# Two weight sums of a Strassen step added by DMA transfers of GpSimd's queue, and the reopened product moved from sixth to third

## The chip, the cores and the metric

One core of one Trainium2 chip runs the whole kernel. The metric is the time of one execution on the device in microseconds; the kernel before has a median of 2315.39 us over 3 runs (2314.23 to 2316.02).

## What is computed

One layer of a hybrid encoder: a modulated RMS norm, two kinds of attention, an output projection, then a second norm and a SwiGLU feed-forward part, all in float32. The change touches the feed-forward part alone:

```python
h2 = rms_norm(x, norm2_g[layer]) * (1 + sc2[:, None]) + sh2[:, None]
ff = (jax.nn.silu(h2 @ w_gate[layer]) * (h2 @ w_up[layer])) @ w_down[layer]
x = x + g2[:, None] * ff
```

Here h2 is 512 x 2048, w_gate and w_up are 2048 x 5632, and w_down is 5632 x 2048.

## The kernel before, in words

Each float32 operand is held as two float32r parts, "hi" and "lo" (lo = full - hi), and each product is three matmuls: hi by hi, hi by lo, lo by hi. ScalarE (ACT) makes the hi part of a weight tile with a Copy, and VectorE (DVE) makes the lo part with a subtraction.

The 5632 columns of w_gate and w_up are done in 44 tiles of 128 (f = 0 to 43). The first 4 (NPL) are done plainly. The other 40 are done by a Strassen-Winograd step that turns eight half products into seven. In the program a tile f >= 4 is a **set** (`product_set` on each engine), and one of its seven products is a **form**, numbered i = 0 to 6 by its place in the set. A form is 8 k-tiles x 3 matmuls = 24 matmuls of 256 columns. Six of the seven activation-side operands are ready-made (H, or the combinations T1 to T4, made once); the weight-side operands are four pieces of 128 x 1024 float32 (512 KB) that SyncE (SP) loads into `raw` slots 0 to 3, and four sums of them.

In a set of the kernel before, DVE makes the four sums in place (`add_raw`, L1783): raw0 += raw2, raw2 += raw3, raw3 += raw0, raw1 += raw3, where each name means the slot's content at that moment. `FORM_RAW` says which raw slot a form is split from, and `FORM_SLOT` where its hi and lo parts go (slots 0 and 1 in W, 3 and 4 in the free half columns of H). Counting semaphores carry the order: `hi_done` and `lo_done` count the halves of the split, `used` counts forms that TensorE (PE) has finished, `summed` counts sums, `raw_in[slot]` landings.

PE takes the forms in the order of the banks P0, P1, S0, S1, T0, P0 again (opened again and added to: the product B21), T1. The combination afterwards is the **u chain** of DVE (L1834 to L1841, five subtractions and additions of 128 x 256): it needs bank T0, and is released by `used` when the T0 form is done. It frees P1 and S1 and leaves the up half and one quarter of the gate to be finished: `c_12` (L1806, needs T1), `silu_11` (ACT L1197, needs the reopened P0), `silu_12` (ACT L1201), and `f_product` (L1811), whose 256 KB result `ftile` GpSimd (POOL) stores to DRAM (`store_f`, L2040). The queue of each engine is written out by hand, so an instruction that waits holds all behind it. In DVE's queue the first split of the next set (`split_form(f, 0)`) stands behind the u chain of the set before.

After the last set the down projection starts (`down_pair`), with the stored f tiles loaded back by POOL (`load_f`, L2049) into the T tiles and H as the last forms free them, and split again (`f_high` on ACT, `f_low` on DVE, L1851).

Of the kernel before, what the change touches and what calls it, by code (L numbers as in the profile page):

```python
# [36 lines left out]
FT = FF // P  # L37
# [6 lines left out]
NPL = 4  # L44
# [37 lines left out]
def layer(nc, x, c, w_ada, b_ada, norm1_g, w_first, w_in, rpb, na_g, lam_p, sub_g, t5, w_out, norm2_g, w_gu, w_down,  # L82
          final_g, out):
    ctx = ExitStack()
    with ctx:
# [3 lines left out]
        def sem(name):  # L89
            return ctx.enter_context(nc.semaphore(name))  # L90
# [138 lines left out]
        gated, f_made, f_hi = sem("gated"), sem("f_made"), sem("f_hi")  # L229
        t_step, t_hi, t_lo = sem("t_step"), sem("t_hi"), sem("t_lo")  # L230
        summed, p1_kept, u_made = sem("summed"), sem("p1_kept"), sem("u_made")
        c12_made, gate_a, gate_b = sem("c12_made"), sem("gate_a"), sem("gate_b")
        f_stored, f_ready = sem("f_stored"), sem("f_ready")
        f_in = [sem(f"f_in{i}") for i in range(7)]
# [24 lines left out]
            return raw_part(slot).rearrange("p (k c) -> p k c", c=HS)  # L259

        FORM_SLOT = (0, 1, 3, 4, 0, 1, 3)
        FORM_RAW = (0, 3, 0, 2, 3, 1, 1)

        def form_no(f, i):
            return NF * f + (STR0 - NF * NPL + i)
# [36 lines left out]
        def landings(slot, group):  # L302

            return 16 * group + 16 * (3, 3, 4, 4, 1 - NK, 1 - NK)[slot]
# [50 lines left out]
        def _(sp):  # L355
# [144 lines left out]
                sp.wait_ge(lo_done, STR0 - 4 + j + 1)  # L500
                load_form(NPL, slot)
            with sp.Fori(NPL + 1, FT) as f:
                sp.wait_ge(summed, 4 * f + (3 - 4 * (NPL + 1)))
                load_form(f, 0)
                sp.wait_ge(lo_done, form_no(f, 4 - NF))
                load_form(f, 2)
                sp.wait_ge(summed, 4 * f + (4 - 4 * (NPL + 1)))
                load_form(f, 3)
                sp.wait_ge(lo_done, form_no(f, 0))
                load_form(f, 1)  # L510
# [5 lines left out]
                cols = down_cols(q, by_row)  # L516
                load(q % 4, w_down[bass.ds(row, 1)].rearrange("a p n -> (a p) n")[:, k0:k0 + cols], cols)

            sp.wait_ge(summed, 4 * FS - 1)
            load_down(0, 0, 0)  # L520
            sp.wait_ge(lo_done, DOWN0)
            load_down(0, 0, 1)
            load_down(0, 0, 2)
            sp.wait_ge(summed, 4 * FS)
            load_down(0, 0, 3)
            for q in range(4, 8):
                sp.wait_ge(lo_done, down_no(0, 0, q - 3))
# [19 lines left out]
        def _(pe):  # L547
# [249 lines left out]
            def form(f, i, bank, rhs, start=True, reopen=False):  # L797

                pe.wait_ge(lo_done, form_no(f, i + 1))
                wh, wl = form_parts(FORM_SLOT[i])  # L800
                out = bank[:, 0:HS]
                for j in range(HALF):
                    hi, lo = [w[:, j // 2, (j % 2) * P:(j % 2) * P + P] for w in (wh, wl)]
                    xh, xl = rhs[j]
                    pe.matmul(out, hi, xh, start=start and j == 0, stop=False, skip_group_check=reopen)  # L805
                    pe.matmul(out, hi, xl, start=False, stop=False, skip_group_check=reopen)  # L806
                    mm = pe.matmul(out, lo, xh, start=False, stop=j == HALF - 1, skip_group_check=reopen)  # L807
                mm.then_inc(used, 1)

            def product_set(f, first=False):  # L810
                pe.wait_ge(gated, NPL) if first else pe.wait_ge(gate_a, f - NPL)
                form(f, 0, Pb[0], B11, reopen=True)
                if first:
                    pe.wait_ge(f_made, NPL)
                    pe.wait_ge(t_lo, 4 * HALF)
                else:
                    pe.wait_ge(u_made, 5 * f - 5 * NPL)
                form(f, 1, Pb[1], T4c)
                form(f, 2, Sb[0], T3c)
                form(f, 3, Sb[1], T1c)  # L820
                form(f, 4, Tb[0], T2c)
                pe.wait_ge(p1_kept, f - (NPL - 1))
                form(f, 5, Pb[0], B21, start=False, reopen=True)
                if not first:
                    pe.wait_ge(c12_made, f - NPL)
                form(f, 6, Tb[1], B22)
# [46 lines left out]
        def _(act):  # L873
# [318 lines left out]
                    split_loaded(NPL, 0, STR0 - 1)  # L1192

            def silu_11(f):
                act.wait_ge(used, form_no(f, 6))
                act.wait_ge(f_made, f)
                act.activation(gate[:, 0:HS], Pb[0][:, 0:HS], ACT.Silu).then_inc(gate_a, 1)  # L1197

# [4 lines left out]
            def product_set(f, first=False):  # L1203
                if not first:
                    split_loaded(f, 0, form_no(f, -2))
                    silu_11(f - 1)
                split_loaded(f, 1, form_no(f, 0 if first else -1))
                split_form(f, 2, summed, 4 * f + (1 - 4 * NPL), form_no(f, 0))
                if not first:
                    silu_12(f - 1)  # L1210
                split_form(f, 3, summed, 4 * f + (2 - 4 * NPL), form_no(f, 0))
                act.wait_ge(used, form_no(f, 1))
                if not first:
                    act.wait_ge(u_made, 5 * f - (5 * NPL + 4))
                act.activation(p1s, Pb[0][:, 0:HS], ACT.Copy).then_inc(p1_kept, 1)
                split_form(f, 4, summed, 4 * f + (3 - 4 * NPL), form_no(f, 1))
                split_loaded(f, 5, form_no(f, 2))
                split_form(f, 6, summed, 4 * f + (4 - 4 * NPL), form_no(f, 3))

            product_set(NPL, True)  # L1220
            with act.Fori(NPL + 1, FT) as f:
# [13 lines left out]
                      down_cols(q, by_row), slot_free)  # L1235

            split_down(0, 0, 0, slot_free=3)
            silu_11(FT - 1)
            f_high(0, 1, 2, 3)
            split_down(0, 0, 1, slot_free=3)  # L1240
            f_high(4, 5)
# [29 lines left out]
        def _(dve):  # L1271
# [541 lines left out]
            def product_set(f, first=False):  # L1813
                g5 = 5 * f - 5 * NPL
                if not first:
                    split_form(f, 0)
                dve.wait_ge(raw_in[2], landings(2, f + GRP0))
                add_raw(0, 0, 2)
                split_form(f, 1)
                if not first:  # L1820
                    c_12(f - 1)
                add_raw(2, 2, 3)
                if not first:
                    f_product(f - 1)
                split_form(f, 2)
                add_raw(3, 3, 0)
                split_form(f, 3)
                split_form(f, 4)
                split_form(f, 5)
                add_raw(1, 1, 3)  # L1830
                split_form(f, 6)
                dve.wait_ge(used, form_no(f, 5))
                dve.wait_ge(p1_kept, f - (NPL - 1))
                dve.tensor_tensor(u2, Tb[0][:, 0:HS], p1s, ALU.subtract).then_inc(u_made, 1)  # L1834
                dve.wait_ge(u_made, g5 + 1)
                dve.tensor_tensor(u3, u2, Sb[0][:, 0:HS], ALU.subtract).then_inc(u_made, 1)
                dve.tensor_tensor(u4, u2, Sb[1][:, 0:HS], ALU.add).then_inc(u_made, 1)
                dve.wait_ge(u_made, g5 + 2)
                dve.wait_ge(f_stored, 16 * f)
                dve.tensor_tensor(ftile[:, 0:HS], u3, Pb[1][:, 0:HS], ALU.add).then_inc(u_made, 1)  # L1840
                dve.tensor_tensor(ftile[:, HS:S], u3, Sb[1][:, 0:HS], ALU.add).then_inc(u_made, 1)  # L1841
# [74 lines left out]
        def _(pool):  # L1916
# [131 lines left out]
                land = triple[2][:, k * S:(k + t1 - t0) * S].rearrange("p (t n) -> p t n", n=S)  # L2048
                pool.dma_start(land, f_d.ap()[t0:t1].rearrange("t p n -> p t n")).then_inc(f_in[r % 7], 16)  # L2049

            with pool.Fori(0, FT - 1) as f:
                store_f(f)
            for r, n in enumerate((DOWN0 - 4, DOWN0 - 3, DOWN0 - 3, DOWN0 - 2, DOWN0, DOWN0, DOWN0)):
                load_f(r, n)
            store_f(FT - 1)
            pool.wait_ge(x_new, KT + 1)
# [54 lines left out]
```

## Time and profile before

| | |
|---|---|
| median of 3 runs | 2315.39 us (2314.23 to 2316.02) |
| the profiled execution | 2317.39 us, its span 2315.5 us |
| PE busy | 2256.2 us (97%) |
| DVE busy | 1578.2 us (68%) |
| ACT busy | 850.6 us (37%) |
| POOL busy | 264.1 us (11%) |
| moved by DMA | 357.02 MB |

"Busy" adds up the instructions of an engine in the profiled execution; the span runs from its first instruction to its last. The matmuls overlap, so PE's share says only that it nearly always had one in hand; how fast it goes is read from the distance between their starts. The stage with the 40 sets runs from about 1009 to 1816 us of the span.

### The profile page before, as it was taken

What the parts mean: (1) busy time and instruction counts of PE and PEld (TensorE: products, weight loads), DVE (VectorE), ACT (ScalarE), POOL (GpSimd) and SP (SyncE); (2) the same over time, 40 slices, a digit from 0 to 9 for tenths busy, and PEclk for the clock granted to TensorE, in tenths of its full rate; (3) what the DMA queues carried; (4) which work ended last, traced back from release to release, by engine and by line L of the source; (5) the groups of instructions that cost most, each with busy time, mean ns of one, the idle gap of its engine ahead of it and who ended that gap; (6) DMA issues with size and microseconds to landing.
All of it is one profiled execution on the core that took longest, in us unless ns stands there. A gap on an engine that the chain in (4) does not pass through costs nothing.

```text
span 2315.5 us, 36235 instructions
## 1 busy us (share of the span) xinstructions
PE 2256.2 (97%) x13160; PEld 1968.7 (85%) x13160; DVE 1578.2 (68%) x2158; ACT 850.6 (37%) x1210; POOL 264.1 (11%) x268
## 2 busy tenths in 40 slices
PE   7989999999999998999999999999999999999997
PEld 5878788777777887799999999999999888888885
DVE  6886777766776898777777777877777632243334
ACT  4224433344445213434444444444434422232221
POOL 4012332200003332000000000000000100001111
PEclk9999999999999998999999999999999999999998
DMA  9896666533442984233333333333333633353333
GB/s 337 285 349 173 199 194 189 188 125 120 163 143 92 353 288 165 91 112 114 110 114 122 122 122 117 113 116 109 117 122 122 225 96 97 94 171 95 99 94 109
DMA packets 126615, 357.02 MB, mean 154 GB/s; under 512 B 12809, under 2 KB 37529, under 8 KB 126049
## 3 DMA queue, kind: packets, MB, share of 16 engines
q1 hardware_dynamic: 115282, 318.03, 41.1%
q0 software_dynamic: 10272, 38.08, 5.5%
q8 instruction: 32, 0.52, 0.1%
q10 hardware_dynamic: 1008, 0.21, 0.1%
q14 instruction: 21, 0.17, 0.0%
HBM read 337.09 MB, written 19.18 MB: 154 GB/s over the span
## 4 chain that ended last, share of the span: by engine, by line
PE 91%; DVE 4%; DMA 2%; ACT 1%; POOL 1%; issue 1%; DVEq 0%; SPq 0%; ACTq 0%; POOLq 0%
PE P L552 7%; PE P L554 7%; PE P L553 7%; PE P L805 5%; PE P L806 5%; PE P L807 5%; PE S L849 3%; PE T L849 3%; PE T L848 3%; PE S L850 3%; PE S L848 3%; PE T L850 3%; PE T L807 3%; PE T L806 3%; PE T L805 3%; PE S L807 3%
## 5 line engine op out<-in xcount | busy, mean ns | idle before, releaser
L1276 DVE TENSOR_TENSOR W_lo<-raw,W_hi 128x1024 fp32r<-128x1024 f32 (+2 forms) x256 | 283.5, 1107 | 331.7 <-ACT W_hi L879 330.9
L879 ACT ACTIVATE W_hi<-raw 128x1024 fp32r<-128x1024 f32 (+2 forms) x256 | 236.8, 925 | 569.9 <-PE T L850 179.5
L552 PE MATMUL P<-H_hi,W_hi 128*128 128x512 f32 x832 | 341.5, 410 | 20.9 <-POOL ident L1948 9.2
L554 PE MATMUL P<-H_hi,W_lo 128*128 128x512 f32 x832 | 326.9, 393 | 0.0
L553 PE MATMUL P<-H_lo,W_hi 128*128 128x512 f32 x832 | 326.4, 392 | 0.0
L1172 ACT ACTIVATE W_hi<-raw 128x1024 fp32r<-128x1024 f32 x160 | 169.2, 1058 | 217.2 <-PE T L807 155.3
L552 PEld LDWEIGHTS P<-H_hi,W_hi 128*128 128x128 f32 x832 | 157.4, 189 | 68.6 <-issue 21.1
L1780 DVE TENSOR_TENSOR W_lo<-raw,W_hi 128x1024 fp32r<-128x1024 f32 x160 | 194.4, 1224 | 3.3 <-ACT W_hi L1172 2.9
L1783 DVE TENSOR_TENSOR raw<-raw 128x1024 f32<-128x1024 f32 x160 | 195.0, 1219 | 0.0
L1172 ACT ACTIVATE H_hi<-raw 128x1024 fp32r<-128x1024 f32 x120 | 127.2, 1060 | 175.5 <-DVE raw L1783 115.2
L554 PEld LDWEIGHTS P<-H_hi,W_lo 128*128 128x128 f32 x832 | 157.1, 189 | 34.3
L553 PEld LDWEIGHTS P<-H_lo,W_hi 128*128 128x128 f32 x832 | 157.7, 190 | 30.7 <-issue 1.9
L805 PE MATMUL S<-T_hi,H_hi 128*128 128x256 f32 x640 | 181.1, 283 | 0.0
L806 PE MATMUL S<-T_lo,H_hi 128*128 128x256 f32 x640 | 181.1, 283 | 0.0
L807 PE MATMUL S<-T_hi,H_lo 128*128 128x256 f32 x640 | 181.1, 283 | 0.0
L806 PE MATMUL P<-H_lo,W_hi 128*128 128x256 f32 x640 | 181.1, 283 | 0.0
L807 PE MATMUL P<-H_hi,W_lo 128*128 128x256 f32 x640 | 181.1, 283 | 0.0
L805 PE MATMUL P<-H_hi,W_hi 128*128 128x256 f32 x640 | 181.1, 283 | 0.0
L1780 DVE TENSOR_TENSOR H_lo<-raw,H_hi 128x1024 fp32r<-128x1024 f32 x120 | 146.6, 1222 | 48.1 <-ACT H_hi L1172 48.1
L2040 POOL DMA_DIRECT2D f_d<-gf x44 | 23.9, 544 | 880.3 <-DVE gf L1811 770.8
L806 PEld LDWEIGHTS P<-H_lo,W_hi 128*128 128x128 f32 x640 | 122.9, 192 | 0.0
L805 PEld LDWEIGHTS P<-H_hi,W_hi 128*128 128x128 f32 x640 | 122.9, 192 | 0.0
(245 smaller groups left out, 5448.0 us busy)
## 6 DMA issues: line engine op xcount, KB each, us to landing
raw<-in_w_gu SPq DMA_DIRECT2D x176, 512.0 KB, 3.3
raw<-in_w_in SPq DMA_DIRECT2D x72, 512.0 KB, 4.3
adar<-in_w_ada SPq DMA_DIRECT2D x72, 512.0 KB, 4.4
att<-in_w_ada SPq DMA_DIRECT2D x32, 1024.0 KB, 10.9
att<-in_w_ada SPq DMA_DIRECT2D x56, 512.0 KB, 4.8
raw<-in_w_down SPq DMA_DIRECT2D x64, 384.0 KB, 3.1
raw<-in_w_down SPq DMA_DIRECT2D x64, 320.0 KB, 2.9
raw<-in_w_out SPq DMA_DIRECT2D x32, 512.0 KB, 4.9
```

The source lines that it names most:

```text
L552: pe.matmul(bank[:, :], wh, xh, start=start, stop=False)
L553: pe.matmul(bank[:, :], wh, xl, start=False, stop=False)
L554: return pe.matmul(bank[:, :], wl, xh, start=False, stop=stop)
L805: pe.matmul(out, hi, xh, start=start and j == 0, stop=False, skip_group_check=reopen)
L806: pe.matmul(out, hi, xl, start=False, stop=False, skip_group_check=reopen)
L807: mm = pe.matmul(out, lo, xh, start=False, stop=j == HALF - 1, skip_group_check=reopen)
L848: pe.matmul(banks[b][:, :], hi, xh, start=(p == 0 and j == 0), stop=False)
L879: act.activation(w_parts(slot)[0][:, 0:cols], raw[:, raw_slot * PW:raw_slot * PW + cols], ACT.Copy).then_inc(hi_done, 1)
L1172: act.activation(form_parts(FORM_SLOT[i])[0], raw_form(FORM_RAW[i]), ACT.Copy).then_inc(hi_done, 1)
L1276: dve.tensor_tensor(lo[:, 0:cols], raw[:, raw_slot * PW:raw_slot * PW + cols], hi[:, 0:cols].bitcast(F32), ALU.subtract).then_inc(lo_done, 1)
L1780: dve.tensor_tensor(lo, raw_form(FORM_RAW[i]), hi.bitcast(F32), ALU.subtract).then_inc(lo_done, 1)
L1783: dve.tensor_tensor(raw_part(dst), raw_part(a), raw_part(b), ALU.add).then_inc(summed, 1)
```

## The change

On POOL, each set now begins with two transfers that add a weight piece from DRAM onto the piece in a raw slot (`accum_op=ALU.add`): raw2 += piece 3 once raw2 has landed, counted by `s1_in`, and raw0 += piece 2 once form 0 of the same set has been split, counted by `s3_in`. The store of the tile before stands behind both. DVE loses two of its four `add_raw`. The reopened product (B21, from raw1) becomes form 2, and the forms of S0, S1 and T0 become 3, 4 and 5; `silu_11` moves into its own set, and the reloads at the end wait for the new form numbers.

```diff
-        FORM_RAW = (0, 3, 0, 2, 3, 1, 1)
+        FORM_RAW = (0, 3, 1, 0, 2, 3, 1)
...
             with sp.Fori(NPL + 1, FT) as f:
-                sp.wait_ge(summed, 4 * f + (3 - 4 * (NPL + 1)))
+                sp.wait_ge(summed, 2 * f + (1 - 2 * (NPL + 1)))
                 load_form(f, 0)
-                sp.wait_ge(lo_done, form_no(f, 4 - NF))
+                sp.wait_ge(lo_done, form_no(f, 5 - NF))
                 load_form(f, 2)
-                sp.wait_ge(summed, 4 * f + (4 - 4 * (NPL + 1)))
+                sp.wait_ge(summed, 2 * f + (2 - 2 * (NPL + 1)))
                 load_form(f, 3)
...
                 form(f, 1, Pb[1], T4c)
-                form(f, 2, Sb[0], T3c)
-                form(f, 3, Sb[1], T1c)
-                form(f, 4, Tb[0], T2c)
                 pe.wait_ge(p1_kept, f - (NPL - 1))
-                form(f, 5, Pb[0], B21, start=False, reopen=True)
+                form(f, 2, Pb[0], B21, start=False, reopen=True)
+                form(f, 3, Sb[0], T3c)
+                form(f, 4, Sb[1], T1c)
+                form(f, 5, Tb[0], T2c)
...
             def silu_11(f):
-                act.wait_ge(used, form_no(f, 6))
+                act.wait_ge(used, form_no(f, 3))
...
                     split_loaded(f, 0, form_no(f, -2))
-                    silu_11(f - 1)
                 split_loaded(f, 1, form_no(f, 0 if first else -1))
-                split_form(f, 2, summed, 4 * f + (1 - 4 * NPL), form_no(f, 0))
+                split_loaded(f, 2, form_no(f, 0))
                 if not first:
                     silu_12(f - 1)
-                split_form(f, 3, summed, 4 * f + (2 - 4 * NPL), form_no(f, 0))
...
-                split_form(f, 4, summed, 4 * f + (3 - 4 * NPL), form_no(f, 1))
-                split_loaded(f, 5, form_no(f, 2))
-                split_form(f, 6, summed, 4 * f + (4 - 4 * NPL), form_no(f, 3))
+                split_form(f, 3, s3_in, 16 * f + (16 - 16 * NPL), form_no(f, 0))
+                split_form(f, 4, s1_in, 16 * f + (16 - 16 * NPL), form_no(f, 1))
+                split_form(f, 5, summed, 2 * f + (1 - 2 * NPL), form_no(f, 2))
+                silu_11(f)
+                split_form(f, 6, summed, 2 * f + (2 - 2 * NPL), form_no(f, 3))
...
                     split_form(f, 0)
-                dve.wait_ge(raw_in[2], landings(2, f + GRP0))
-                add_raw(0, 0, 2)
                 split_form(f, 1)
                 if not first:
                     c_12(f - 1)
-                add_raw(2, 2, 3)
+                split_form(f, 2)
                 if not first:
                     f_product(f - 1)
-                split_form(f, 2)
+                split_form(f, 3)
                 add_raw(3, 3, 0)
-                split_form(f, 3)
                 split_form(f, 4)
                 split_form(f, 5)
                 add_raw(1, 1, 3)
                 split_form(f, 6)
-                dve.wait_ge(used, form_no(f, 5))
+                dve.wait_ge(used, form_no(f, 6))
...
-            with pool.Fori(0, FT - 1) as f:
+            def add_weights(f):
+
+
+                def add(slot, other, landed):
+                    pool.dma_start(raw_part(slot), w_gu[bass.ds(4 * f + other, 1)].rearrange("a p n -> (a p) n"),
+                                   accum_op=ALU.add).then_inc(landed, 16)
+
+                pool.wait_ge(raw_in[2], landings(2, f + GRP0))
+                add(2, 3, s1_in)
+                pool.wait_ge(lo_done, form_no(f, 1))
+                add(0, 2, s3_in)
+
+            with pool.Fori(0, NPL - 1) as f:
                 store_f(f)
-            for r, n in enumerate((DOWN0 - 4, DOWN0 - 3, DOWN0 - 3, DOWN0 - 2, DOWN0, DOWN0, DOWN0)):
+            with pool.Fori(NPL, FT) as f:
+                add_weights(f)
+                store_f(f - 1)
+            for r, n in enumerate((DOWN0 - 3, DOWN0 - 2, DOWN0 - 3, DOWN0 - 1, DOWN0, DOWN0, DOWN0)):
                 load_f(r, n)
```

`form_no(f, n)` as a value of `used` or `lo_done` means that forms 0 to n-1 of set f are through.

On PE, in the loop over the sets, the last part of a set: the T0 form (operand T, weights in W), then the reopened P form, then the T1 form (T<-H_hi: weights and operand both in H). Before:

```order
L805 MATMUL T<-T_hi,W_hi 128x256 [waits lo_done]
...
L799 REGISTER_ALU [waits p1_kept]
L805 MATMUL P<-H_hi,W_hi 128x256 [waits lo_done]
...
L799 REGISTER_ALU [waits c12_made]
L805 MATMUL T<-H_hi 128x256 [waits lo_done]
```

Now, from the reopened P form on:

```order
L800 REGISTER_ALU [waits p1_kept]
L806 MATMUL P<-H_hi 128x256 [waits lo_done]
...
L806 MATMUL S<-T_hi,H_hi 128x256 [waits lo_done]
...
L806 MATMUL S<-T_hi,W_hi 128x256 [waits lo_done]
...
L806 MATMUL T<-T_hi,W_hi 128x256 [waits lo_done]
...
L800 REGISTER_ALU [waits c12_made]
L806 MATMUL T<-H_hi 128x256 [waits lo_done]
```

Two forms stood between the end of T0's form and the first form of the next set; now there is one.

On DVE, the end of the loop body (the u chain, after which the body begins anew with the first split and what follows it). Before, the end:

```order
L1833 REGISTER_ALU [waits used]
L1834 TENSOR_TENSOR tail<-T,tail 128x256 [waits p1_kept]
L1835 ISA
L1836 TENSOR_TENSOR tail<-tail,S 128x256 [waits u_made]
L1837 TENSOR_TENSOR tail<-tail,S 128x256
L1838 REGISTER_ALU
L1839 REGISTER_ALU [waits u_made]
L1840 TENSOR_TENSOR gf<-tail,P 128x256 [waits f_stored]
L1841 TENSOR_TENSOR gf<-tail,S 128x256
```

and the beginning of the body, before:

```order
L1780 TENSOR_TENSOR W_lo<-raw,W_hi 128x1024 [waits hi_done]
L1817 ISA
L1783 TENSOR_TENSOR raw<-raw 128x1024 [waits raw_in2]
L1778 REGISTER_ALU
L1780 TENSOR_TENSOR W_lo<-raw,W_hi 128x1024 [waits hi_done]
```

and now:

```order
L1780 TENSOR_TENSOR W_lo<-raw,W_hi 128x1024 [waits hi_done]
L1778 REGISTER_ALU
L1780 TENSOR_TENSOR W_lo<-raw,W_hi 128x1024 [waits hi_done]
L1804 ISA
L1805 ISA [waits used]
L1806 TENSOR_TENSOR tail<-T,tail 128x256 [waits u_made]
```

The end of the body is the same five operations in the same place of DVE's queue; only the form that its wait names has moved. From the beginning, the first sum is gone.

On POOL, the loop over the sets, now (before, it held the last three rows and the loop's own):

```order
L2052 ISA [waits raw_in2]
L2052 DMA raw<-in_w_gu 128x1024
L2057 ISA
L2052 ISA [waits lo_done]
L2052 DMA raw<-in_w_gu 128x1024
L2037 ISA [waits f_made]
L2037 DMA f_d<-gf 128x512
L2062 REGISTER_ALU
```

Two waits and two transfers now stand ahead of the store.

## Rows read from the trace of the kernel before

**Rows 1.** Busy time by stretch: us; busy us of PE, PEld, DVE, ACT, POOL; clock, DMA share, GB/s

```profile
1014.00:1100.00 86.00, 86.00 (x719) 86.00 (x718) 69.34 (x78) 36.69 (x44) 2.17 (x4) 1.00 0.36 122
1100.00:1780.00 680.00, 680.00 (x5670) 680.00 (x5668) 527.53 (x609) 283.06 (x338) 18.43 (x34) 1.00 0.35 116
1830.00:1900.00 70.00, 70.00 (x310) 57.98 (x309) 27.36 (x37) 21.08 (x32) 0.53 (x1) 1.00 0.38 119
```

**Rows 2.** PE's waits from 1009 to 1830 us: waited for, us in total, times, longest

```profile
PE P L805 <- DVE W_lo L1780: 0.3, 1, 0.3
```

**Rows 3.** Groups of instructions by form, 1100 to 1780 us (33.7 sets)

```profile
L1783 DVE TENSOR_TENSOR raw<-raw 128x1024 f32<-128x1024 f32 x136 | 165.7, 1219 | 0.0
```

**Rows 4.** PE's timeline in one set: last T0 matmul, first reopened P, first T1

```profile
1306.48 0.28 PE L807 MATMUL T<-T_hi,W_lo 128*128 128x256 f32 x1
1306.60 0.28 PE L805 MATMUL P<-H_hi,W_hi 128*128 128x256 f32 x1
...
1309.48 0.28 PE L805 MATMUL T<-H_hi 128*128 128x256 f32 x1
```

**Rows 5.** DVE's timeline in the same set: u chain, first split of the next set

```profile
1306.89 0.43 DVE L1834 TENSOR_TENSOR tail<-T,tail 128x256 f32<-128x256 f32 x1 [2.84 <-PE T L807]
1307.35 0.42 DVE L1836 TENSOR_TENSOR tail<-tail,S 128x256 f32<-128x256 f32 x1
...
1308.35 0.41 DVE L1841 TENSOR_TENSOR gf<-tail,S 128x256 f32<-128x256 f32 x1
1308.68 1.22 DVE L1780 TENSOR_TENSOR W_lo<-raw,W_hi 128x1024 fp32r<-128x1024 f32 x1
```

**Rows 6.** DVE's timeline where the first set begins

```profile
1010.27 1.22 DVE L1783 TENSOR_TENSOR raw<-raw 128x1024 f32<-128x1024 f32 x1
1011.41 1.22 DVE L1780 TENSOR_TENSOR W_lo<-raw,W_hi 128x1024 fp32r<-128x1024 f32 x1
```

**Rows 7.** PE's timeline at the same place

```profile
1012.16 0.28 PE L807 MATMUL P<-H_hi,W_lo 128*128 128x256 f32 x1
1012.77 0.35 PE L805 MATMUL P<-T_hi,W_hi 128*128 128x256 f32 x1 [0.33 <-DVE W_lo L1780]
1012.97 0.28 PE L806 MATMUL P<-T_lo,W_hi 128*128 128x256 f32 x1
```

**Rows 8.** ACT's and DVE's timelines: a sum, the hi half of its split, the lo half

```profile
1300.39 1.22 DVE L1783 TENSOR_TENSOR raw<-raw 128x1024 f32<-128x1024 f32 x1
1301.72 1.06 ACT L1172 ACTIVATE H_hi<-raw 128x1024 fp32r<-128x1024 f32 x1 [2.50 <-DVE raw L1783]
1302.82 1.23 DVE L1780 TENSOR_TENSOR H_lo<-raw,H_hi 128x1024 fp32r<-128x1024 f32 x1 [1.21 <-ACT H_hi L1172]
```

**Rows 9.** DVE's and POOL's timelines: the product of a tile and its store

```profile
1314.13 0.69 DVE L1811 TENSOR_TENSOR gf<-gf 128x512 f32<-128x512 f32 x1
1315.46 0.54 POOL L2040 DMA_DIRECT2D f_d<-gf  x1 [19.61 <-DVE gf L1811]
```

**Rows 10.** DMA issues over the whole span: KB each, median us from issue to landing

```profile
raw<-in_w_gu SPq DMA_DIRECT2D x176, 512.0 KB, 3.3
f_d<-gf POOLq DMA_DIRECT2D x44, 256.0 KB, 2.3
T_f<-f_d POOLq DMA_DIRECT2D x5, 1024.0 KB, 8.0
X<-in_x POOLq DMA_DIRECT2D x4, 1024.0 KB, 6.0
att<-t_d POOLq DMA_DIRECT2D x8, 448.0 KB, 3.8
```

**Rows 11.** DVE's and POOL's timelines where the last set ends and down begins

```profile
1812.68 0.95 DVE L1276 TENSOR_TENSOR W_lo<-raw,W_hi 128x768 fp32r<-128x768 f32 x1
1814.61 2.50 DVE L1851 TENSOR_TENSOR T_lo<-T_f,T_hi 128x512 fp32r<-128x512 f32 x4 [0.98 <-ACT T_hi L1228]
...
1805.30 0.78 POOL L2049 DMA_DIRECT2D T_f<-f_d  x1 [5.45 <-PE S L807]
```

**Rows 12.** PE's timeline there: first matmuls of down

```profile
1816.36 0.40 PE L848 MATMUL S<-T_hi,W_hi 128*128 128x512 f32 x1
1816.59 0.40 PE L849 MATMUL S<-T_lo,W_hi 128*128 128x512 f32 x1
```

**Rows 13.** How long POOL is busy with an issue: duration ns min/median/max

```profile
L2040 POOL DMA_DIRECT2D f_d<-gf x44: 539/542/604, 946.1 to 1822.7; - x44
```

More of the change, by code:

```diff
@@ L231, in layer @@
         summed, p1_kept, u_made = sem("summed"), sem("p1_kept"), sem("u_made")
+        s3_in, s1_in = sem("s3_in"), sem("s1_in")
         c12_made, gate_a, gate_b = sem("c12_made"), sem("gate_a"), sem("gate_b")
@@ L517, in load_down @@
                 load(q % 4, w_down[bass.ds(row, 1)].rearrange("a p n -> (a p) n")[:, k0:k0 + cols], cols)
-            sp.wait_ge(summed, 4 * FS - 1)
+            sp.wait_ge(summed, 2 * FS - 1)
             load_down(0, 0, 0)
@@ L523, in _ @@
             load_down(0, 0, 2)
-            sp.wait_ge(summed, 4 * FS)
+            sp.wait_ge(summed, 2 * FS)
             load_down(0, 0, 3)
@@ L1237, in _ @@
             split_down(0, 0, 0, slot_free=3)
-            silu_11(FT - 1)
             f_high(0, 1, 2, 3)
```

## The prediction

> **What bounds the kernel now.** I read the busy time by stretch first. Through the stage of the 40 sets PE is busy all of the time at a granted clock of 1.00, which is the 2.4 GHz level, while DVE has 78% and the DMA engines 35% [rows 1]. PE starts 5670 matmuls in 680 us, one every 0.120 us [rows 1], so a form of 24 takes 2.88 us (the timeline agrees: 1309.48 - 1306.60 [rows 4]) and a set of 168 takes 20.16 us. Next PE's waits: from 1009 to 1830 us it waited once, 0.3 us [rows 2]. So PE's queue alone sets the time here, and nothing that unburdens DVE can shorten a set. The change leaves PE's 168 matmuls as they are; it can only leave the stage alone or put waits into it. The question is how near each supplier now comes to PE.
>
> **Sums taken off DVE.** Two `add_raw` a set at 1.22 us [rows 3] are 2.4 us less for DVE, in every one of 40 sets. They lie beside PE's work, so I cost them at nothing. One of them counts once: where the first set begins, the sum and the split behind it run from 1010.27 to 1012.63 [rows 6], and PE starts its next form at 1012.77 where its rhythm of 0.12 behind 1012.16 would have had 1012.28, and the matmul after it at 1012.97 instead of 1012.40 [rows 7]. Without the sum that is gone: **-0.6 us**.
>
> These rows also give the price of a late split. It ended 0.35 us after PE wanted to start (1012.63 against 1012.28), and PE lost 0.57. So lost time = lateness + 0.22 us.
>
> **The u chain, moved nearer to the next set.** This is the term that decides. The chain waits for T0's form. Before, that form was the fifth of seven, with two forms (5.76 us) ahead of the next set; now it is the sixth, with one (2.88 us). DVE's queue is in order, and behind the chain stands the lo half of the next set's first split, for which PE's next form waits. What that takes, counted from the start of the form behind T0's: the chain starts 0.29 us later (1306.89 - 1306.60 [rows 4, 5]), its five operations take 1.79 (1308.68 - 1306.89), and the split 1.22 [rows 5]: 0.29 + 1.79 + 1.22 = 3.30 us. Before, 5.76 were there, a margin of 2.46. Now there are 2.88, so the split is 0.42 us late and PE loses 0.42 + 0.22 = **0.64 us at each border between sets, 39 times: +25.0 us**. The hi half on ACT is no help and no harm: its slot is free after the fifth form, as before, and it is done before DVE comes to it. Bounds: if only the lateness counted, 39 x 0.42 = 16 us; if the chain met another 0.25 us of waiting, 39 x 0.89 = 35 us.
>
> **The sum in raw0, added by POOL.** It can be issued only when form 0 has been split, and form 3 is made from it. I count from the end of form 0's split, which now also starts PE's set, 0.22 us later in effect. PE wants form 3 at 0.22 + 8.64 = 8.86. Back from there: 0.14 from a split's end to PE (1012.77 - 1012.63), 1.22 for the lo half, 0.04 between, 1.06 for the hi half, 0.11 from a result to ACT [rows 6, 7, 8]. It must have landed by 6.3. POOL starts an issue 0.64 us after what it waited for (1315.46 - 1314.82 [rows 9]). That leaves **5.6 us from issue to landing**. No row shows an adding transfer. Below stands the plain 512 KB load from the same tensor, 3.3 us; above, a POOL transfer of 1024 KB, 6.0 us, and one of 8.0 where the DMA engines were crowded [rows 10], since an addition has to read the 512 KB in SBUF as well as those in DRAM. POOL's 448 KB took 3.8 [rows 10]. The rate of this queue between 448 and 1024 KB, (6.0 - 3.8) / 576 KB, makes 512 KB 4.0 us. Reading twice as much would bring it to 6.0; with half of the second reading hidden beside the first it is 5.0. I take 5.0, nearer to the 448 KB row because these transfers fall where SP's queue rests, and so cost the wait nothing; the ends are 3.3 and 8.0, which is +0 and 39 x 2.4 = +94 us.
>
> The Trainium skill (DMA: Bandwidth & Descriptors, Anatomy of one DMA) puts a transfer of this queue at 2.0 us and bytes over 436 GB/s: 3.2 us for 512 KB and 4.4 for twice as much; the trace has 6.0 where it gives 4.4 for 1024 KB, so it runs low here. By it the sum of terms would be the same, with 1.2 us to spare.
>
> **The sum in raw2.** Issued when piece 2 of the next set has landed. That load now waits for form 4's split, some 9 to 10 us into a set, so it lands near 13, and even at 8.0 us the sum is there by 22, while form 4 is wanted at 11.5 + 20.8 = 32. Nothing.
>
> **Other moves.** POOL's store stands behind two more issues of about 0.54 us [rows 13]; both are out before `f_product`, and the u chain asks for the store 17 us later. Nothing. The kept copy of P0 must be ready for form 2 at 5.76: form 0 ends at 2.88 and ACT has only `silu_12` before it. Nothing, with over 2 us of cover. `silu_11` leaves the set border, where nobody waited for it. SP's four loads come between 8.5 and 14.5 us into a set and land 3.3 later; the last, raw1, near 18, is wanted after the next border. Nothing. The traffic rises by 1 MB a set, from 35% to some 50 to 60% of the DMA engines.
>
> **The end of the stage.** Behind the last u chain come the first down split (0.95 us for 768 columns) and f tiles at 0.6 each (four in 2.50) [rows 11]. Down's first tile is ready 0.29 + 1.79 + 0.95 + 0.62 = 3.65 us after the last form starts, against 2.88: lost 0.77 + 0.22 = 1.0. Tiles 4 and 5 stand behind one more split and cost about 0.5. The reload of the first four tiles goes out one form (2.88 us) later than at 1805.30; with 8.0 us it lands about 0.2 us before down begins, and may cost another 0.5. Together **+2.0** (0.4 to 5).
>
> **Sum.** 25.0 + 2.0 - 0.6 = +26.4 us. Against the profiled execution, 2317.39, that is 2343.8; the median of the runs lies 2.0 lower, so **2341.8 us**. Its own range is 2332 to 2352.
>
> **Rivals.**
> *The sum in raw0 comes late.* A second wait then joins the first in every set, at form 3. For: the addition's own rate is unknown, and only 0.6 us lie between my 5.0 and the 5.6. At twice the plain load, 6.6 us, PE loses 1.0 more a set: +39, 2381 us. At 8.0 it is 2436.
> *The chain hides after all.* If the chain and the split together took under 2.7 us, for instance because one of the five operations' own waits (0.46 us from the first to the second against 0.33 for the others) is shorter now, the border would cost nothing: 2316 to 2320. Against it: the rows before show the same five operations with the same inputs.
> *Faster.* PE's matmuls of 256 columns start every 0.120 us, while those of 512 columns in down start every 0.226 (70 / 310 [rows 1]; 0.23 [rows 12]), half of which is 0.113. If the difference came from DVE's sums reading and writing SBUF beside PE, taking away half of them could give back up to 168 x 0.007 = 1.2 us a set, 47 us in all, and with the u chain's price 2294. It decides where the distance is shorter while DVE rests. But from 1304.05 to 1306.89 DVE rested [rows 5, 8], and the starts at 1306.48 and 1306.60 in that rest are 0.12 apart all the same [rows 4]. The Trainium skill (TensorE: Matmul & The Clock Gate, Back-to-back issue gap) has columns over 2.4 GHz plus 2.5 ns, 0.109 us for 256; the trace has 0.120.
> That the change doesn't do what it says is out: DVE's order has two sums a set fewer and POOL's two transfers more.
>
> **Chances.** Forecast 0.55; late sum 0.30; hidden chain 0.10; faster 0.05. A difference under 0.2% (4.6 us) can't be told from none. The first two are slower: 0.85. The range runs from 2327, below the forecast's own low end by some of a partly hidden chain, to 2390, which takes in the late sum up to 6.8 us.
>
> **What the profile will show.** Right: in PE's waits a row for the lo split of W with 39 entries of about 0.4 us; sets 20.8 us apart; DVE idle before the u chain for longer than the 2.84 us of before [rows 5]; the adding transfers at about 5 us. Wrong: PE waiting for H's lo half (form 3), which is the late sum; or sets at 20.16; or a distance of matmuls under 0.12.

## The result, and the profile after

| | before | after |
|---|---|---|
| median of 4 runs | 2315.11 us (2314.23 to 2316.02) | 2368.38 us (2358.28 to 2374.32) |
| the profiled execution | 2317.39 us, span 2315.5 | 2366.78 us, span 2365.2 |

The ratio is 1.0226 (95% interval 1.0189 to 1.0262): the changed kernel is 53 us slower. Its runs also spread over 16 us, where those of before lie within 2. The prediction was 2341.8 us, its range 2327 to 2390.

The table of busy time by stretch for the changed kernel, in the same 680 us as in [rows 1] (us; busy us of PE, PEld, DVE, ACT, POOL; clock, DMA share, GB/s):

```profile
1100.00:1780.00 680.00, 653.38 (x5333) 642.60 (x5333) 425.54 (x510) 260.66 (x317) 73.43 (x95) 1.00 0.66 159
```

PE started 5333 matmuls in the stretch instead of 5670: it got through 6% less work, at the same granted clock of 1.00. DVE fell from 528 to 426 us, and the DMA engines' share rose from 0.35 to 0.66. Where PE's time went is in its waits from 1009 to 1880 us (waited for, us in total, times, longest), which were one of 0.3 us before [rows 2]:

```profile
PE S L806 <- DVE H_lo L1780: 20.2, 21, 1.5
PE P L806 <- DVE W_lo L1780: 12.3, 39, 0.3
PE S L849 <- DVE T_lo L1848: 0.9, 2, 0.7
PE P L806 <- DVE H_lo L1780: 0.9, 3, 0.5
```

The second row is the forecast wait, at the border between sets, 39 times. The first is a wait of another kind: the S bank with its weights split into H is form 3, the one made from the raw0 that GpSimd's queue adds to. It came 21 times, up to 1.5 us each. The last row, 3 times and 0.9 us in all, is form 2 (the P bank with its weights in H), which is split from the raw1 that SP loads.

PE's timeline at a border and, further on in the same set, at form 3:

```profile
1328.63 0.28 PE L808 MATMUL T<-H_hi,H_lo 128*128 128x256 f32 x1
1329.22 0.39 PE L806 MATMUL P<-H_hi,W_hi 128*128 128x256 f32 x1 [0.32 <-DVE W_lo L1780]
1329.44 0.28 PE L807 MATMUL P<-H_lo,W_hi 128*128 128x256 f32 x1
...
1339.25 0.39 PE L806 MATMUL S<-T_hi,H_hi 128*128 128x256 f32 x1 [1.13 <-DVE H_lo L1780]
```

In its rhythm of 0.12 PE would have started at 1328.75 and 1328.87; it started at 1329.22 and 1329.44, so the border took 0.57 us. The wait recorded in brackets, 0.32, is shorter: it counts from the recorded end of the matmul before (1328.63 + 0.28 = 1328.91) and not from when the next should have started, and the second matmul starts 0.22 behind the first instead of 0.12.

The starts of the u chain show how this adds up. DVE's timeline (three sets):

```profile
1284.70 0.43 DVE L1831 TENSOR_TENSOR tail<-T,tail 128x256 f32<-128x256 f32 x1 [2.36 <-PE T L808]
...
1305.42 0.43 DVE L1831 TENSOR_TENSOR tail<-T,tail 128x256 f32<-128x256 f32 x1 [2.30 <-PE T L808]
...
1326.16 0.43 DVE L1831 TENSOR_TENSOR tail<-T,tail 128x256 f32<-128x256 f32 x1 [2.29 <-PE T L808]
...
1348.27 0.43 DVE L1831 TENSOR_TENSOR tail<-T,tail 128x256 f32<-128x256 f32 x1 [2.02 <-PE T L808]
```

The first two distances are 20.72 and 20.74 us: a set of before (20.16) and a border (0.57). The third is 22.11: 1.4 us more, the late form 3. (The first matmul of a set starts 3.1 us behind the start of the chain before it, here at 1329.22, and in the set before at 1308.49.) From 1024.51, the first chain, to 1838.96, the 39th, are 814.45 us. At 20.16 a set 38 sets are 766.1; borders take 38 x 0.57 = 21.7, which leaves **26.7 us for late sums** (with the three waits at form 2 among them). In 16 of the 38 distances there is none (20.72 to 20.84 us), in the others 0.4 to 1.8 us.

What the sum in raw0 waited for is in the timelines of POOL and ACT around that late set. POOL's:

```profile
1324.32 0.87 POOL L2052 DMA_DIRECT2D raw<-in_w_gu  x1 [11.40 <-DMA raw<-in_w_gu]
1329.80 0.87 POOL L2052 DMA_DIRECT2D raw<-in_w_gu  x1 [4.61 <-DVE W_lo L1780]
```

ACT's:

```profile
1332.22 1.06 ACT L1173 ACTIVATE H_hi<-raw 128x1024 fp32r<-128x1024 f32 x1 [4.94 <-DMA raw<-in_w_gu]
...
1336.88 1.06 ACT L1173 ACTIVATE H_hi<-raw 128x1024 fp32r<-128x1024 f32 x1 [3.02 <-DMA raw<-in_w_gu]
```

The addition into raw2 went out at 1324.32, the one into raw0 at 1329.80, and its hi split started at 1336.88, when it had landed: about 7.1 us after its issue. The split at 1332.22 is form 2's, which waited for SP's load of raw1. All three transfers were under way together. From issue to landing these two additions took (the smaller is raw0's, the larger raw2's):

```profile
DMA to landing us min/median/max: 7.1/7.5/8.0
```

So raw2's was still in flight for 2.5 us when raw0's went out. The rows of DMA issues, over the whole span (KB each, median us from issue to landing), against 3.3 for SP's before [rows 10]:

```profile
raw<-in_w_gu SPq DMA_DIRECT2D x176, 512.0 KB, 4.3
raw<-in_w_gu POOLq DMA_DIRECT2D x80, 512.0 KB, 7.4
```

The 7.4 is the median over both places. Taken apart in the trace, by the order of issue, the additions into raw2 took 5.4/7.9/8.9 us (min/median/max) and those into raw0, for which form 3 waits, 5.2/6.2/7.5, where I had taken 5.0 and had found room for 5.6. Over the 40 of them, what goes beyond 5.6 us adds up to 29 us, close to the 26.7 lost. When raw0's addition went out, raw2's had 2.4 us still to go at the median.

### The profile page after: what moved, and what is told of

Read it like the earlier page. It is cut to its first block, busy times and chain, and to the rows that moved or that the text cites. A ratio compares the mean times of both kernels' runs of the same rounds, so it can differ in the third digit from the quotient of the medians.

```text
span 2365.2 us, 36358 instructions
## 1 busy us (share of the span) xinstructions
PE 2272.3 (96%) x13160; PEld 1971.7 (83%) x13160; DVE 1483.3 (63%) x2078; ACT 843.2 (36%) x1210; POOL 334.1 (14%) x348
## 4 chain that ended last, share of the span: by engine, by line
PE 75%; DMA 9%; DVE 8%; issue 4%; ACT 2%; POOL 2%; DVEq 0%; POOLq 0%; ACTq 0%; SPq 0%
PE P L553 7%; DMA raw<-in_w_gu 7%; PE P L555 7%; PE P L554 7%; PE S L806 3%; PE T L850 3%; PE T L851 3%; PE T L849 3%; PE S L849 3%; PE S L850 3%; PE S L851 3%; PE S L808 3%; PE S L807 3%; PE P L806 2%; PE T L553 2%
## 5 line engine op out<-in xcount | busy, mean ns | idle before, releaser
L553 PEld LDWEIGHTS P<-H_hi,W_hi 128*128 128x128 f32 x832 | 157.4, 189 | 68.5 <-issue 20.7
L554 PEld LDWEIGHTS P<-H_lo,W_hi 128*128 128x128 f32 x832 | 157.7, 190 | 30.5 <-issue 1.9
L2052 POOL DMA_DIRECT2D raw<-in_w_gu x80 | 69.6, 869 | 590.0 <-DMA raw<-in_w_gu 390.9
L1285 DVE CUSTOM_DVE_ANT_0 adar<-adar,csb 128x1024 f32<-128x1024 f32 x72 | 95.8, 1345 | 35.1 <-DMA adar<-in_w_ada 35.0
L806 PE MATMUL S<-T_hi,H_hi 128*128 128x256 f32 x320 | 92.9, 290 | 20.3 <-DVE H_lo L1780 20.2
L806 PE MATMUL P<-H_hi,W_hi 128*128 128x256 f32 x320 | 94.5, 295 | 12.3 <-DVE W_lo L1780 12.3
L553 PE MATMUL T<-H_hi,W_hi 128*128 128x512 f32 x256 | 99.9, 390 | 1.5 <-DVE W_lo L1276 1.2
L555 PE MATMUL T<-H_hi,W_lo 128*128 128x512 f32 x256 | 99.6, 389 | 0.0
L554 PE MATMUL T<-H_lo,W_hi 128*128 128x512 f32 x256 | 99.6, 389 | 0.0
L1783 DVE TENSOR_TENSOR raw<-raw 128x1024 f32<-128x1024 f32 x80 | 97.5, 1218 | 0.0
```

The source lines that it names most:

```text
L553: pe.matmul(bank[:, :], wh, xh, start=start, stop=False)
L554: pe.matmul(bank[:, :], wh, xl, start=False, stop=False)
L555: return pe.matmul(bank[:, :], wl, xh, start=False, stop=stop)
L1783: dve.tensor_tensor(raw_part(dst), raw_part(a), raw_part(b), ALU.add).then_inc(summed, 1)
```

## The experiments

Each kernel ran beside the kernel before on the same chip. Times are medians; the interval is that of the ratio to the kernel before.

### e1: the new order alone

Edit: the forms in the changed order, all four sums on DVE, no transfer from GpSimd's queue but the store. (Here and below the waits of SP and ACT that count sums change to match; those lines are not shown.)

```diff
                 if not first:
                     split_form(f, 0)
+                dve.wait_ge(raw_in[2], landings(2, f + GRP0))
+                add_raw(0, 0, 2)
                 split_form(f, 1)
                 if not first:
                     c_12(f - 1)
+                add_raw(2, 2, 3)
                 split_form(f, 2)
...
-                pool.wait_ge(raw_in[2], landings(2, f + GRP0))
-                add(2, 3, s1_in)
-                pool.wait_ge(lo_done, form_no(f, 1))
-                add(0, 2, s3_in)
+                pass
```

> The new order of the forms alone: the reopened product third, T0's form sixth, all four sums on DVE and no adding transfer. Theory (the u chain stands too near to the next set): 39 borders lose the 0.57 us that the changed kernel shows where nothing else is late (sets 20.73 us apart instead of 20.16), so about +22 us, 2337 us, and no wait at the S forms. Rival (all of the loss comes from the adding transfers): within 3 us of the kernel before, 2315.

Measured: 2339.30 us, ratio 1.0101 (1.0084 to 1.0118), 24.0 us over the kernel before. PE's waits:

```profile
PE P L806 <- DVE W_lo L1780: 12.5, 40, 0.3
PE S L849 <- DVE T_lo L1851: 1.2, 2, 0.7
```

No wait at an S form is left. 40 waits for W's lo half are the 39 borders and the one where the first set begins, which was there before. So the border is a cost of the order of the forms, with nothing of the transfers in it: 39 x 0.57 = 22.2 of the 24.0 us; the rest is at the end of the stage.

### e2, e3, e7, e8: which transfer, and what of it

e2: both transfers as plain copies (neither sum is computed).

```diff
-                    pool.dma_start(raw_part(slot), w_gu[bass.ds(4 * f + other, 1)].rearrange("a p n -> (a p) n"),
-                                   accum_op=ALU.add).then_inc(landed, 16)
+                    pool.dma_start(raw_part(slot), w_gu[bass.ds(4 * f + other, 1)].rearrange("a p n -> (a p) n")).then_inc(landed, 16)
```

> The changed kernel with the two transfers of GpSimd's queue as plain copies of the same pieces to the same places (the sums raw0 + piece 2 and raw2 + piece 3 are not computed). Theory A (the addition in the transfer is what makes it slow): issue to landing falls from 7.4 to about 4.0 us, no wait at form 3, the u chain's 22 us stay: 2337 us. Theory B (the second queue's traffic alone is enough): landing stays over 6 us and the time near 2368.

e3: only the sum in raw0 on GpSimd's queue.

```diff
                     c_12(f - 1)
+                dve.wait_ge(raw_in[2], landings(2, f + GRP0))
+                add_raw(2, 2, 3)
                 split_form(f, 2)
...
-                pool.wait_ge(raw_in[2], landings(2, f + GRP0))
-                add(2, 3, s1_in)
                 pool.wait_ge(lo_done, form_no(f, 1))
                 add(0, 2, s3_in)
```

> The changed kernel with only the sum in raw0 added by GpSimd's queue; DVE adds the one in raw2. Theory (the two adding transfers get in each other's way and in that of the raw1 load): the remaining one takes about 5.2 us as in the best sets of the changed kernel, no wait at form 3, 2337 us. Rival (one adding transfer is slow by itself): it takes 7 us, PE waits about 1.5 us at form 3 in every set, over 2380 us.

e7 and e8: both transfers, one of them a plain copy (`ALU.bypass`): in e7 the one into raw0, in e8 the one into raw2 (the sum of the plain one is not computed).

> The changed kernel with the transfer into raw0 a plain copy (that sum is not computed) and the one into raw2 adding. Theory (an addition takes 5.3 us alone and only an adding neighbour or the raw1 load stretches it): the adding one 6 us or more beside SP's loads, the plain one about 4.5, no wait at form 3: 2339 us. Rival (the slow part is whatever comes second in the queue, adding or not): form 3 waits as in the changed kernel, near 2360 us.

> The changed kernel with the transfer into raw2 a plain copy (that sum is not computed) and the one into raw0 adding. Theory (it takes an adding neighbour to make the sum in raw0 late): as e3_s3_only, about 5.3 us from issue to landing in the sets, PE waits at form 3 in few sets if any, 2340 us. Rival (the second transfer's traffic does it): form 3 waits in half of the sets, 2355 us or more.

Landing is from issue to landing, min/median/max in us, for each of the two places apart.

| | adds in transfers | time, us | ratio (interval) | landing, raw2 | landing, raw0 | PE's waits at form 3 |
|---|---|---|---|---|---|---|
| after | both | 2368.38 | 1.0226 (1.0189 to 1.0262) | 5.4/7.9/8.9 | 5.2/6.2/7.5 | 21 |
| e2 | none | 2339.31 | 1.0102 (1.0085 to 1.0119) | 3.4/6.8/7.8 | 3.4/3.5/5.0 | 0 |
| e3 | raw0 | 2340.13 | 1.0107 (1.0090 to 1.0124) | none | 5.2/5.4/5.6 | 1 |
| e7 | raw2 | 2340.45 (one run) | | 5.4/7.8/8.7 | 3.5/3.6/5.1 (plain) | 0 |
| e8 | raw0 | 2339.94 (one run) | | 3.4/6.7/8.0 (plain) | 5.1/5.4/5.9 | 1 |

Every one of the four falls back to the time of e1. So the two times 512 KB on the second queue are no trouble by themselves (e2), and one addition is none either, on whichever slot (e3, e7, e8). Two additions a set, placed as the changed kernel has them, are.

The two columns tell more. The transfer into raw2 is slow even as a plain copy with no addition anywhere (6.8 us in e2), and SP's load of raw1, which is in flight with it, rises too: 4.2 us at the median in e1, 6.6 in e2, 7.7 in the changed kernel. In e8 raw2's plain copy had 1.0 us still to go when raw0's addition went out, and that landed in 5.4 us all the same. e7 tests less than it seems: where raw0's plain copy lands after 3.6 us, the next sum and the loads behind it come earlier, raw2's transfer goes out 7.4 us ahead of raw0's instead of 5.4, and only 0.4 us of the two overlap.

In the changed kernel itself 10 of the 40 additions into raw0 had no load of SP beside them at any time, and 7 of these took over 5.6 us (up to 7.4). So SP's loads are not needed to make it late. The DMA queues from 1100 to 1780 us say what an addition costs (packets, MB, share of the 16 engines' time); the row of GpSimd's queue in e1, which has the stores alone:

```profile
q0 software_dynamic: 2631, 8.62, 3.3%
```

in e2, with two plain copies a set:

```profile
q0 software_dynamic: 12064, 43.00, 17.8%
```

in e3, with one addition a set:

```profile
q0 software_dynamic: 7261, 25.55, 18.5%
```

and in the changed kernel, with two:

```profile
q0 software_dynamic: 11520, 41.09, 31.3%
```

Less the stores' 3.3%, the 66 plain copies of e2 took 14.5% of 680 us: 1.5 us of all 16 engines each. The 33 additions of e3 took 15.2%: 3.1 us each. An adding transfer of the same bytes keeps the engines busy twice as long, and two that overlap need over 6 us of the engines together, with SP's loads among them. That makes it plausible that raw0's addition is stretched when raw2's is still in flight; how the engines divide their time between the two is not shown.

### e10: the same two additions, the other one first

Edit to the changed kernel:

```diff
                 pool.wait_ge(raw_in[2], landings(2, f + GRP0))
-                add(2, 3, s1_in)
                 pool.wait_ge(lo_done, form_no(f, 1))
                 add(0, 2, s3_in)
+                add(2, 3, s1_in)
```

> The changed kernel with the two adding transfers issued back to back, the one into raw0 first and the one into raw2 behind it. Theory (the sum in raw0 is late because the other addition is still on the DMA engines when it is issued; each takes some 3 us of all 16): the first now lands in 5.2 to 5.8 us, PE has no waits at form 3, the second lands 8 us after its own issue, just in time for form 4 or up to 0.5 us late: 2339 to 2355 us. Rival (two additions in flight share the engines evenly, whichever came first): both take 8 us, form 3 is late by 2.4 us in every set, over 2420 us.

Measured: 2341.12 us, ratio 1.0108 (1.0092 to 1.0123). Late sums are gone in all but 5 of 39 distances between sets, with both additions still there. (PE waited twice at form 3, 0.8 us, and twice at form 4, 1.8 us, which is made from raw2.) POOL's timeline of one set:

```profile
1091.65 1.78 POOL L2052 DMA_DIRECT2D raw<-in_w_gu  x2 [16.88 <-DVE W_lo L1780]
```

and ACT's:

```profile
1097.09 1.06 ACT L1173 ACTIVATE H_hi<-raw 128x1024 fp32r<-128x1024 f32 x1 [2.38 <-PE P L808]
1100.05 2.01 ACT L1173 ACTIVATE W_hi<-raw 128x1024 fp32r<-128x1024 f32 x2 [1.91 <-DMA raw<-in_w_gu]
```

The two landed as follows (the smaller is raw0's):

```profile
DMA to landing us min/median/max: 5.4/6.6/7.8
```

The split made from raw0 started 5.4 us after the first issue, when that addition had landed. (The row names PE, but of PE this split needs only that the set before is done, and that was some 6 us earlier.) The one made from raw2 started 8.4 us after the same moment, 7.8 after its own issue. Over all sets the first took 5.2/5.4/6.3 us and the second 7.1/7.3/9.4. The one issued first was not held up by the one behind it, though they were in flight together. The addition into raw0 goes out at the same place of a set as in the changed kernel, 0.6 us behind the set's first matmul. So what made raw0's sum late there is that raw2's had been issued ahead of it and was still in flight. Both are in one queue; whether two queues would do the same was not run.

### e4, e5, e6: the split ahead of the u chain

e4 and e5 take the first split of the next set (`split_form(f + 1, 0)`) from behind the u chain to ahead of it in DVE's queue. In e4 the transfer into raw0 is also held to about where the changed kernel has it.

```diff
-                if not first:
-                    split_form(f, 0)
                 split_form(f, 1)
...
                 split_form(f, 6)
+                if last:
+                    split_down(0, 0, 0)
+                else:
+                    split_form(f + 1, 0)
                 dve.wait_ge(used, form_no(f, 6))
...
                 pool.wait_ge(lo_done, form_no(f, 1))
+                pool.wait_ge(used, form_no(f, 0))
                 add(0, 2, s3_in)
```

(the last addition in e4 alone)

> The changed kernel with the first split of the next set ahead of the u chain in DVE's queue (the border's stall is taken away), and with the transfer into raw0 held until TensorE has finished the set before, so that it starts at about the same place of a set as in the changed kernel. Theory (two separate terms, 22 us of the u chain and some 27 us of late sums): the 22 us go, the late sums stay or grow by about 0.3 us a late set: 2343 to 2352 us, with no wait at a set's first form. Rival (the late sums are a consequence of the border's stall): about 2316 us.

Measured: 2367.52 us, ratio 1.0226 (1.0209 to 1.0243). This missed what was expected: the border's 22 us are gone, and the time is still that of the changed kernel. PE's waits from 1005 to 1870 us:

```profile
PE S L806 <- DVE H_lo L1780: 32.8, 33, 1.7
PE P L806 <- DVE H_lo L1780: 3.4, 10, 0.7
PE S L849 <- DVE T_lo L1856: 1.7, 1, 1.7
```

No wait for W's lo half is left, 33 at form 3 have come in place of 21, and 10 at form 2 (SP's load of raw1) in place of 3. From the first chain to the 39th are 813.9 us, 47.8 over 38 sets of 20.16. So the two terms don't add. The border's stall had moved PE's wish for form 3 back by 0.57 us. Counted from the u chain, that wish now comes 0.57 earlier and the issue only 0.26 earlier (3.39 us behind the chain's start instead of 3.65), so the room is 0.3 us less, 5.3 instead of 5.6. The additions into raw0 also took longer, 6.6 us at the median instead of 6.2. What they take beyond 5.3 adds up to 50 us, near the 47.8; that this is the whole account is my estimate. Why they took longer is not shown.

e5, without that hold:

> The changed kernel with the first split of the next set ahead of the u chain in DVE's queue, and nothing else moved: the transfer into raw0 waits for that split alone, so it goes out some 3 us earlier in a set. Theory (both losses come from a split that stands behind the u chain): sets 20.16 us apart, the sum in raw0 lands in time even at 7.4 us, PE has no waits at W's or H's lo half: 2314 to 2318 us. Rival (two adding transfers a set are too much for the DMA engines wherever they stand): waits at form 3 stay, over 2340 us.

Measured: 2319.38 us (11 runs), ratio 1.0013 (1.0003 to 1.0022). Sets are 20.16 us apart. All that PE waits for from 1005 to 1870 us, in the profiled execution (2324.08 us, the slowest of the 11), is

```profile
PE S L849 <- DVE T_lo L1856: 3.1, 1, 3.1
```

The additions into raw0 and raw2 are in flight together here too, even longer (4.5 us at the median), and they are no quicker: 7.8 us at the median into raw2 and 6.9 into raw0. But the one into raw0 goes out when form 0 is split, and that is now before the u chain (POOL's timeline):

```profile
1086.30 0.88 POOL L2059 DMA_DIRECT2D raw<-in_w_gu  x1 [8.31 <-DMA raw<-in_w_gu]
1089.26 0.88 POOL L2059 DMA_DIRECT2D raw<-in_w_gu  x1 [2.08 <-DVE W_lo L1780]
```

DVE's timeline there:

```profile
1087.39 1.23 DVE L1780 TENSOR_TENSOR W_lo<-raw,W_hi 128x1024 fp32r<-128x1024 f32 x1 [1.75 <-ACT W_hi L1173]
1089.27 0.43 DVE L1833 TENSOR_TENSOR tail<-T,tail 128x256 f32<-128x256 f32 x1 [0.65 <-PE T L808]
```

The issue now falls together with the start of the chain; in the changed kernel it was 3.64 us behind it (1329.80 - 1326.16). With that, 7 us are quick enough, and the longest into raw0, 7.7, too.

e6 is e1 with the early split, all sums on DVE.

> The new order of the forms with all four sums on DVE, as in e1_order, and the first split ahead of the u chain. Theory (the whole 24 us of e1_order is the split behind the chain): 2315 to 2318 us, sets 20.16 us apart. Rival (the new order costs in another way, at the p1 copy or the end of the stage): 2325 to 2339 us.

Measured: 2318.63 us (10 runs), ratio 1.0010 (1.0001 to 1.0019). Its waits in the stage are 2.4 us at down's beginning and the 0.3 at the first set. Each against the kernel before of its own session, e1 lost 24.0 us and e6 loses 2.6, so the early split takes away 21.4, and what stays is the end of the stage again.

### e9: the last set in the old order

e5, with set 43 as in the kernel before: T0's form fifth, its four sums on DVE, and the reloads as early.

```diff
+        LAST_RAW = (0, 3, 0, 2, 3, 1, 1)
...
+                if last:
+                    form(f, 2, Sb[0], T3c)
+                    form(f, 3, Sb[1], T1c)
+                    form(f, 4, Tb[0], T2c)
+                    pe.wait_ge(p1_kept, f - (NPL - 1))
+                    form(f, 5, Pb[0], B21, start=False, reopen=True)
...
-            for r, n in enumerate((DOWN0 - 3, DOWN0 - 2, DOWN0 - 3, DOWN0 - 1, DOWN0, DOWN0, DOWN0)):
+            for r, n in enumerate((DOWN0 - 4, DOWN0 - 3, DOWN0 - 3, DOWN0 - 2, DOWN0, DOWN0, DOWN0)):
```

> e5_early_split with the last of the 40 sets in the order of the kernel before (its four sums on DVE, T0's form fifth, the reloads of the f tiles as early as before). Theory (what e5_early_split still loses, 3 us, is the reload of the first f tiles that goes out one form later, and TensorE's wait for them where down begins): that wait of 3.1 us goes, 2315 to 2317 us, at or just below the kernel before. Rival (the 3 us are spread over the sets or lie ahead of them): it stays at 2319.

Measured: 2315.79 us (11 runs, against 2315.65 for the kernel before in the same session), ratio 1.0003 (0.9994 to 1.0012). Its list of PE's waits from 1005 to 1870 us is empty. Against the kernel before of their own sessions, e5 lies 3.4 us above and e9 0.1; the 3.2 us between them are the end of the stage. It is the best version with the additions, 53 us faster than the changed kernel, and it can't be told from the kernel before. It undoes three things at once in the last set (T0's place, the sums, the reloads), so which of them the 3.2 us were is not shown; in e5 ACT's first split of a reloaded tile waited for the landing, which points at the reloads:

```profile
1815.20 2.20 ACT L1229 ACTIVATE T_hi<-T_f 128x512 fp32r<-128x512 f32 x4 [2.23 <-DMA T_f<-f_d]
```

## Why the prediction was right, and where it was not

**The bound.** Right. PE's queue alone sets the stage's time. DVE lost two sums a set and nothing came of it: e9, where PE has no waits left and 39 sets run without those two sums, takes as long as the kernel before.

**The u chain.** Right in mechanism, place and count, and a little too large: 0.64 us a border forecast, 0.57 measured, so 22 instead of 25 us. e1 shows it without any transfer, and e6 takes it away by moving one instruction in DVE's queue.

**The first set.** As forecast: in e1 PE waits 40 times for W's lo half and in the changed kernel 39. At 0.6 us it is below what the runs can tell.

**The end of the stage.** Forecast at +2.0 us. In e1 PE waits 1.2 us there by its records and 1.8 us of the total are left for it; in e5 it waits 3.1. The size holds within the bounds given.

**The sum in raw0.** Its room was reckoned well, its landing was not. The prediction said that an addition takes 5.0 us, "nearer to the 448 KB row because these transfers fall where SP's queue rests", against room for 5.6, and gave the late sum a chance of 0.30. Alone it takes 5.4 us, not 5.0 (e3), which still just fits: e3 has one late set. In the changed kernel it takes 6.2 at the median and up to 7.5.

**The sum in raw2: "Nothing".** This step failed, and it is what made the other late. It asked only whether form 4 would wait for this sum, and there it was right: no wait at form 4 came. It did not ask which other transfer this one is in flight with. Raw2's load waits for form 4's split, which ends 10.6 us into a set and not at 9 to 10. It lands 4.3 us after its issue and not 3.3, so the addition goes out at 15.8 (1324.32 - 1308.49) and not just behind 13. And it takes 8 us, so it is in flight until 2.5 us after the one into raw0 has been issued. e10 shows that the order is what counts: with raw0's first, that one is back at 5.4 us. The line "Nothing" on SP's four loads passed by something too: the load of raw1 rose from 3.2 to 7.7 us, it was in flight beside raw0's addition in most sets, and form 2 waited for it three times (0.9 us).

**The total.** The forecast case was 2341.8; e1, e2 and e3, which have it with at most one late sum, measure 2339 to 2340. The changed kernel is at 2368 because the rival, a late sum, came true beside it, for 27 us in the profiled execution. The loss is 53 us where the sum of terms had 26.4, so the time lies in the stated range through the rival that the range took in, and the case held most likely (0.55) is not what happened. That the rival's size fits is in part luck. It was priced as a slow addition, the same in every set; what came was an addition that is quick enough alone and is stretched by its neighbour, in 22 of 38 distances between sets, by 0.4 to 1.8 us. Where the 16 us between the changed kernel's runs come from is open: e1 and e2, without late sums, lie within 4 and 1.2, but e4, with more late sums, lies within 4 as well.

**Faster by closer matmuls.** The rival has fallen: with half of DVE's sums gone, matmuls start 0.12 us apart as before (e5: 5669 in the 680 us in which the kernel before starts 5670).

## What to carry to other kernels

On a stage where one engine is never idle, work taken off another engine is worth nothing, and the change is to be read for what it brings nearer to that engine: count from the event that releases each step through everything ahead of it in its own in-order queue, and move the one instruction that the bounding engine waits for ahead of those that nobody waits for. A transfer must be checked twice, for who waits for it, and for which other transfers are in flight with it; issue first the one that is needed first. When an early wait holds back the engine that a later transfer must be ready for, the two don't add: taking the early one away can hand its time to the later one (e4), so cure them together. And a median over transfers of one queue can mix two kinds: take apart the one that is waited for.

## What the runs showed of the hardware that I had not expected

- An adding transfer of 512 KB kept the 16 DMA engines busy for 3.1 us, a plain one for 1.5. Its issue kept POOL busy for 0.87 us, against 0.53. From issue to landing it took 5.4 us with no other transfer into a raw slot from its queue in flight (e3). With the end of another addition beside it, it took 6.2 at the median (changed kernel), with the end of a plain copy 5.4 (e8).
- A plain copy of GpSimd's queue and a load of SP's queue, both 512 KB and in flight together, were both slow: 6.8 us at the median for the copy into raw2 and 6.6 for the load of raw1 (e2), where that load took 4.2 with no GpSimd copy beside it (e1) and the copy into raw0 3.5 (e2).
- Of two additions issued 0.6 us apart from one queue the first landed as if alone, in 5.4 us at the median, and the second took 7.3 (e10). GpSimd's store behind them rose to a median of 5.3 us, against 2.3.
- SP's loads of raw slots rose from a median of 3.2 us to 4.2 in the stage of e1 as well, where GpSimd's queue carries only the stores. The new order alone does that, by bringing the loads closer together, or so I take it; it cost nothing there.
- A late matmul costs PE more than its recorded wait: 0.57 us where the record has 0.32, since the record begins at the end of the matmul before, and 0.10 us of the 0.57 come between the late matmul and the one behind it.
